# A 48-part projection in a fused two-network kernel: transposing each part by itself instead of twelve parts at a time

## The reference, cut to what matters

```python
def ada_chunks(cvec, w, b):          # cvec: (1024,), w: (1024, 6144), one w per layer
    m = jax.nn.silu(cvec) @ w + b
    return jnp.split(m[..., None, :], 6, axis=-1)
```

## Time and profile before

| | |
|---|---|
| median of 3 runs | 2052.83 us (2052.32 to 2052.91) |
| profiled execution: time, span | 2052.83 us, 2051.0 us |
| PE, PEld busy | 1939.6 us (95%), 1647.2 us (80%) |
| DVE, ACT busy | 1289.0 us (63%), 914.8 us (45%) |
| mean granted TensorE clock | 0.978 of full |

### The profile page before, as it was taken

How to read it: one execution, slowest core, us unless ns; L and a number is a source line. 1 busy time by engine, 2 the same in 40 slices (tenths; PEclk the granted TensorE clock), 3 DMA queues, 4 the chain that set the end, 5 groups by cost and what they waited for, 6 DMA issues and landing times.

```text
span 2051.0 us, 28815 instructions
## 1 busy us (share of the span) xinstructions
PE 1939.6 (95%) x12002; PEld 1647.2 (80%) x12002; DVE 1289.0 (63%) x1732; ACT 914.8 (45%) x1266; POOL 14.2 (1%) x17
## 2 busy tenths in 40 slices
PE   6999978999999999699999998999999989999998
PEld 5788857888788888488779876988888879678997
DVE  4775775776567658667566445665554356757775
ACT  5334534434543353443264345543333254655553
POOL 0000000000000000000000100000000000000000
PEclk9999988999999999899999999999999999999999
DMA  6675444666466644467433311132222222113552
GB/s 264 246 259 194 166 160 163 224 250 228 164 246 226 226 173 176 165 230 265 164 144 131 136 52 52 62 123 83 93 96 99 103 83 86 59 56 130 187 191 95
DMA packets 45488, 320.62 MB, mean 156 GB/s; under 512 B 5040, under 2 KB 5168, under 8 KB 6960
## 3 DMA queue, kind: packets, MB, share of 16 engines
q1 hardware_dynamic: 38592, 270.09, 36.7%
q10 hardware_dynamic: 6768, 48.69, 6.3%
HBM read 317.72 MB, written 1.05 MB: 155 GB/s over the span
## 4 chain that ended last, share of the span: by engine, by line
PE 85%; DVE 9%; ACT 3%; issue 2%; DMA 1%; ACTq 0%; POOLq 0%; POOL 0%; SPq 0%; DVEq 0%
PE ps L521 82%; DVE s_wl L1869 2%; DVE s_big L2147 2%; ACT s_wh L1223 1%; PE ps L858 1%; PE ps L721 0%; DVE s_xx L1869 0%; DVE s_tmp L1956 0%; DMA s_ca<-in_c_all 0%; PE ps L698 0%; DVE s_X L2037 0%; ACT s_xx L1223 0%; DVE s_big L2021 0%; DVE s_tmp L2018 0%; DMA s_big<-in_bias 0%
## 5 line engine op out<-in xcount | busy, mean ns | idle before, releaser
L521 PE MATMUL ps<-s_xx,s_wh 128*128 128x512 f32 (+1 forms) x3328 | 903.5, 349 | 17.4 <-DVE s_wl L1869 16.0
L1869 DVE TENSOR_TENSOR s_wl<-s_raw,s_wh 128x2048 fp32r<-128x2048 f32 x215 | 492.2, 2290 | 334.1 <-ACT s_wh L1223 333.9
L521 PE MATMUL ps<-s_xx,s_wl 128*128 128x256 f32 (+1 forms) x2208 | 671.2, 304 | 7.2 <-DVE s_wl L1869 6.5
L521 PEld LDWEIGHTS ps<-s_xx,s_wh 128*128 128x128 f32 x3328 | 584.1, 191 | 109.9 <-DVE s_wl L1869 19.7
L1223 ACT ACTIVATE s_wh<-s_raw 128x2048 fp32r<-128x2048 f32 x215 | 409.0, 1907 | 158.0 <-PE ps L521 157.6
L521 PEld LDWEIGHTS ps<-s_xx,s_wl 128*128 128x128 f32 x2208 | 421.9, 191 | 25.7 <-DVE s_wl L1869 6.9
L521 PE MATMUL ps<-s_wh,s_hl 128*128 128x512 f32 (+1 forms) x608 | 233.8, 385 | 5.9 <-DVE s_tmp L1956 3.5
L521 PE MATMUL ps<-s_wl,s_hh 128*128 128x512 f32 (+1 forms) x608 | 231.4, 381 | 0.0
L521 PE MATMUL ps<-s_wh,s_hh 128*128 128x512 f32 (+1 forms) x608 | 231.2, 380 | 0.0
L521 PE MATMUL ps<-s_wh,s_xx 128*128 128x256 f32 x928 | 177.6, 286 | 0.0
L521 PEld LDWEIGHTS ps<-s_wh,s_xx 128*128 128x128 f32 x928 | 148.6, 192 | 3.8 <-issue 3.8
(11 more groups left out here) (228 smaller groups left out, 1690.3 us busy)
## 6 DMA issues: line engine op xcount, KB each, us to landing
s_big<-in_w_ada ACTq DMA_DIRECT2D x46, 1024.0 KB, 5.1
s_raw<-in_ffn_gate SPq DMA_DIRECT2D x44, 1024.0 KB, 4.9
s_raw<-in_ffn_up SPq DMA_DIRECT2D x44, 1024.0 KB, 4.8
s_raw<-in_ffn_down SPq DMA_DIRECT2D x44, 1024.0 KB, 4.7
s_raw<-in_w_up SPq DMA_DIRECT2D x44, 1024.0 KB, 4.8
s_raw<-in_w_down SPq DMA_DIRECT2D x22, 1024.0 KB, 4.8
s_raw<-in_w_in SPq DMA_DIRECT2D x18, 1024.0 KB, 4.8
s_raw<-in_w_in_ab SPq DMA_DIRECT2D x10, 1024.0 KB, 4.8
```

Source lines behind the costliest of these rows:

```text
L521: return pe.matmul(o, lhsT, rhs, start=start, stop=stop, skip_group_check=True)
L1869: dve.tensor_tensor(wide(wl, u), raw[:, u % SLOTS, :].rearrange("p (k n) -> p k n", k=8), f32(wide(wh, u)), SUB).then_inc(*w_low.tick(u))
```

## The change

Each part is now transposed by itself. `fill(b)` takes a bank (6 in a feed-forward, the next of the rotation in a mixer) and starts and ends its own accumulation there. `cpad` is a buffer of its own, 32 columns wide, and the slice no longer moves. ACT copies each part to `tmp[:, 5]`, after waiting until the columns of the part before have been taken from it. Directly behind fill f, PE runs `ada_columns(f - 1)`: two matmuls of 128x128 by 128x2 with the constant `pick` (four ones per column). `ada_columns(47)` stays where the last one was, and now also waits for `modulation(0)`. `modulation(0)` waits only for the columns of part 46. The matrix `pick`, and the DVE instruction that made it, are gone. In the mixers `bank()` is called once more for each fill, on PE and on ACT, and `mixer_bank` lists the fills in their places.

```diff
@@ allocation and banks
-        pick = sb("pick", [128, 24])
+        cpad = sb("cpad", [128, 8, 32])
...
-        cpad = big[:, 10816:11248].rearrange("p (k n) -> p k n", k=8)
...
-             ("in", 2), ("rope", "qm"), ("in", 3), ("rope", "km"), "pool", "mean", "stat", "rs"] +
-            [("out", j) for j in range(4)])}
+            [("in", 7), ("in", 8), ("in", 0), ("in", 4), ("in", 5), ("rope", "qd"), ("in", 6), ("rope", "kd"), ("fill", 0),
+             ("fill", 1), ("in", 1), ("in", 2), ("rope", "qm"), ("in", 3), ("rope", "km"), ("fill", 2), "pool",
+             ("fill", 3), ("fill", 4), ("fill", 5), ("fill", 6), "mean", ("fill", 7), "stat", "rs", ("fill", 8)] + [("out", j) for j in range(4)])}
@@ tensor
-            def ada_columns(g):
-
-                pe.wait_ge(*half[g])
-                pe.wait_ge(*picked[0])
+            def ada_columns(f):
+                pe.wait_ge(*half[f])
+                if f == 47:
+                    pe.wait_ge(*modulated[0])
                 for c in range(2):
-                    o = ps[7][:, 48 * g:48 * g + 48].rearrange("p (f c s) -> p f c s", c=2, s=2)[:, :, c, :]
-                    m = mm(o, tmp[:, 5, 128 * c:128 * c + 128], pick[:, :].rearrange("p (f s) -> p f s", s=2), True, True)
-                m.then_inc(*product.tick(("columns", g)))
-
-            def fill():
-
-
+                    m = mm(ps[7][:, 4 * f + 2 * c:4 * f + 2 * c + 2], tmp[:, 5, 128 * c:128 * c + 128], const("pick"),
+                           True, True)
+                m.then_inc(*product.tick(("columns", f)))
+
+            def fill(b):
                 f = fills[0]
                 fills[0] += 1
-                g, i = f // 12, f % 12
+                fill_bank[f] = b
+                pe.wait_ge(*ada_in[f % 2][f])
+                claim(b)
                 if f == 0:
                     pe.wait_ge(*gated["c"])
-                if g and i == 0:
-                    ada_columns(g - 1)
-                pe.wait_ge(*ada_in[f % 2][f])
                 w = ada_buf(f).rearrange("p (k n) -> p k n", k=8)
                 for k in range(8):
                     rows = slice(32 * (k % 4), 32 * (k % 4) + 32)
-                    m = mm(ps[7][rows, 256:512], cpad[:, k, 22 - 2 * i:54 - 2 * i], w[:, k, :], i == 0 and k < 4,
-                           i == 11 and k >= 4)
+                    m = mm(ps[b][rows, 0:256], cpad[:, k, :], w[:, k, :], k < 4, k >= 4)
                 m.then_inc(*product.tick(("fill", f)))
+                freed[b] = half[f]
+                if f:
+                    ada_columns(f - 1)
...
                     if j in ADA_AT[s]:
-                        fill()
+                        fill(6)
                 if s == ("ffn2", 1):
-                    ada_columns(3)
+                    ada_columns(47)
@@ scalar, fill()
-                if f % 12 == 11:
-                    g = f // 12
-                    if g:
-                        act.wait_ge(*product["columns", g - 1])
-                    act.activation(tmp[:, 5, 0:256], ps[7][:, 256:512], ACT.Copy).then_inc(*half.tick(g))
+                if f:
+                    act.wait_ge(*product["columns", f - 1])
+                act.activation(tmp[:, 5, 0:256], ps[fill_bank[f]][:, 0:256], ACT.Copy).then_inc(*half.tick(f))
@@ vector
-                dve.wait_ge(*product["columns", 3])
+                dve.wait_ge(*product["columns", 47 if l else 46])
...
-            dve.tensor_reduce(pick[:, :], const("ident").rearrange("p (g j) -> p j g", g=4)[:, 0:24, :], AX, ADD).then_inc(*picked.tick(0))
```

More of the change, by code:

```diff
@@ L153, in program @@
         normed, hidden, resid, tapped = (signal(n) for n in ("normed", "hidden", "resid", "tapped"))
-        added, picked = signal("added"), signal("picked")
+        added = signal("added")
         roped, masked, row_max, divided = (signal(n) for n in ("roped", "masked", "row_max", "divided"))
@@ L296, in program @@
         k_places = [big[:, 10240:10752], big[:, 10752:11264], cb[:, 768:1280], cb[:, 1280:1792]]
+        fill_bank = {}
         mixer_bank = {x: 6 - n % 2 for n, x in enumerate(
-            [("in", 7), ("in", 8), ("in", 0), ("in", 4), ("in", 5), ("rope", "qd"), ("in", 6), ("rope", "kd"), ("in", 1),
-             ("in", 2), ("rope", "qm"), ("in", 3), ("rope", "km"), "pool", "mean", "stat", "rs"] +
-            [("out", j) for j in range(4)])}
+            [("in", 7), ("in", 8), ("in", 0), ("in", 4), ("in", 5), ("rope", "qd"), ("in", 6), ("rope", "kd"), ("fill", 0),
+             ("fill", 1), ("in", 1), ("in", 2), ("rope", "qm"), ("in", 3), ("rope", "km"), ("fill", 2), "pool",
+             ("fill", 3), ("fill", 4), ("fill", 5), ("fill", 6), "mean", ("fill", 7), "stat", "rs", ("fill", 8)] + [("out", j) for j in range(4)])}
         ropes_flat = ropes[:, :, :].rearrange("p a t -> p (a t)")
@@ L924, in mixer @@
                 for _ in range(2):
-                    fill()
+                    fill(bank())
                 for i in range(6):
@@ L1437, in mixer @@
                 for _ in range(2):
+                    bank()
                     fill()
@@ L1514, in ctx_squares @@
                 act.wait_ge(*ctx_in[0])
-                act.wait_ge(*product["columns", 3])
+                act.wait_ge(*product["columns", 47])
                 for b in range(4):
@@ L1813, in scalar @@
             act.wait_ge(*cleared["cpad"])
-            act.activation(cpad[:, :, 22:24], v("c", 0, 16).rearrange("p (k s) -> p k s", s=2), ACT.Silu).then_inc(
+            act.activation(cpad[:, :, 0:2], v("c", 0, 16).rearrange("p (k s) -> p k s", s=2), ACT.Silu).then_inc(
                 *gated.tick("c"))
```

## The result

The changed kernel took 2071.14 us (median of 4 runs, 2065.65 to 2072.36) beside 2052.57 us for the kernel before on the same chip (2050.53 to 2052.91): 1.0088 times as long, 95% interval 1.0067 to 1.0107. It is slower, by 18.6 us where 13.1 were forecast. Its profiled execution took 2070.3 us with a span of 2068.3, against 2051.0 in the earlier trace rows. PE was busy for 28.6 us more and idle for 11.3 us less, which makes up the 17.3 us by which the span grew.

A forecast was written before the change was run, and what follows sets the result against it. PE, busy for 95% of the span, was taken as the bound. The terms 14.0 + 5.4 - 6.0 - 0.3 = +13.1 us on 2052.83 us gave 2065.9 us, 0.64% slower, range 2059 to 2074.

The forecast's parts named there:

- Part 1: Feed-forwards: 28 more pairs of short matmuls on PE at 0.50 us each, +14.0 us, bounds 9.8 and 15.7.
- Cheap pairs: Rival: a pair's loads hide under running passes, 0.1 us a pair in feed-forwards; +1.9, 2054.7 us; chance 0.08.
- faster: Rival: pairs' loads fit the loader's idle time and copies stay hidden; -6.3, 2046.5 us; chance 0.03.
- Part 2: Five places in each mixer where fills and pairs add time: 2.7 us a mixer, 5.4 for both, bounds 2.8 and 11.6.
- (c): Mixers: one more pair on the way from fill to values, 0.5 us a mixer, up to 1.0 at half clock.
- (d): Mixers, behind fill 13: ACT waits for the pair and copies first, 0.9 us a mixer, up to 1.4.
- (e): Mixers: output projection starts right behind fill 14, so the pair adds 0.5 us a mixer, up to 1.0.
- (a): Mixers: fill 7 waits for the rope's bank, ahead of the scores; 0.1 us a mixer, bounds 0 and 1.5.
- (b): Mixers: pool product moves behind rope "km" on one bank, making DVE late; 0.7 us a mixer, bounds 0 and 0.9.
- the mixers' banks bind: Rival: fills 7 and 8 wait for copies, then PE, DVE, ACT wait at half clock; +19.3, 2072.1 us; chance 0.15.
- Part 3: Before the last feed-forward's down units: PE's 3.52 us wait and the half clock behind it go, -6.0 us.
- Part 4: At the start: DVE's 0.32 us for `pick` leaves the chain, -0.3 us, bounds -0.35 and 0.

The follow-up runs named there:

- e6: Changed kernel without the 29 pairs behind fills in feed-forwards, halves still copied: 2059.24 us, ratio 1.0046 to the kernel before.
- e2: Kernel before with only the end changed: `modulation(0)` waits for fill 47, the last pair waits for `modulation(0)`; no added pairs: 2043.92 us, ratio 0.9968.
- e9: Changed kernel with the pair in front of the fill instead of behind it in feed-forwards: 2062.99 us, ratio 1.0069 to the kernel before.
- e5: Changed kernel with each pair behind a fill in feed-forwards made twice, 29 more pairs: 2078.28 us, ratio 1.0139 to the kernel before.
- e3: Changed kernel with every fill moved to bank 7, out of the mixers' rotation of banks: 2063.43 us, ratio 1.0061 to the kernel before.
- e4: Changed kernel with one bank number skipped in each mixer, ahead of the mean's bank: 2067.71 us, ratio 1.0088 to the kernel before.
- e7: Changed kernel without the 18 pairs behind fills in the mixers: 2059.20 us, ratio 1.0045 to the kernel before.
- e12: Kernel before with the end changed as in e2 and DVE's `pick` sum moved to step 3 of the first feed-forward: 2042.77 us, ratio 0.9969.
- e1: Changed kernel with only the wait put back: `modulation(0)` waits for the last pair of columns again: 2074.20 us, ratio 1.0124 to the kernel before.
- e11: Kernel before measured once more, no edit: 2050.05 us, ratio 1.0005.
- e10: Changed kernel measured once more, no edit: 2063.95 us, ratio 1.0076 to the kernel before.

## Why the prediction was right, and where a size was off

The forecast, slower by 13.1 us to 2065.9, had the right sign, and the median lies in its range. That isn't all merit: the mixers cost more than the forecast's own high bound for them, and part 1 and a pitch that nobody foresaw took 3 us off the other side. On its own terms:

**Part 1, 14.0 us: right, a little high.** At a pitch of 0.353 us the four feed-forwards gained 2.23, 3.59, 3.19 and 193.68 - 189.75 = 3.93 us, in all 12.9, for 28 more pairs: 0.46 each, by the rows 0.45 where 0.50 was taken and 0.35 to 0.56 were the bounds. (Of the 3.93, 0.31 isn't the pairs': e6, without pairs, has 190.06, while e2 is back at the quicker pitch behind its last fill.) The row with eight passes in 1.00 us was a good guide; a pair ahead of a fill costs the 0.34 that the lower bound gave (e9). "Cheap pairs" and "faster", which need 0.1 and 0.05 us a pair, are out: doubling showed 0.45 each (e5). A pass of the pair thus takes 0.112 us at full clock. The Trainium skill ("TensorE: Matmul & The Clock Gate", section "LDWEIGHTS (loading the stationary operand)") puts a load at its columns over 1.2 GHz, 107 ns for 128; the trace agrees within 5% at full clock. At half clock a pair holds PE for 0.88 us, twice as long. The same page's 25 ns floor, which the prediction set beside this rule, doesn't bind here.

**The pitch: not foreseen.** In the first profile ffn2_1 ran at 0.347 us, 1.9 us less than its like. 12.9 - 1.9 - 5.95 = +5.1 is what the four feed-forwards together show. It held through a stage only where pairs stand behind fills, so it looks like an effect of the change that comes in some executions; what sets it isn't shown.

**Part 2, 5.4 us: the term that was too small.** The sum of its five places was the step that failed. The mean over profiles is +12.2 us and the first profile had +14.2, where the high bound was 11.6. (Its low bound doesn't follow from its terms either: (c), (d) and (e) alone have 0.5 + 0.9 + 0.5 = 1.9 a mixer, 3.8 and not 2.8 for both.) DVE has the same instructions in each mixer of every run, so a mixer can be cut at them. The table has the forecast for both mixers and what was measured: the mean of the six profiles with the changed code less that of the four with the code of before. Lines are those of the kernel before.

```
place    the stretch ends with                   forecast  measured
(a)      L2018 for rope "km"                        0.2      +0.94
(b)      L2204, which reads the pool product        1.4      +1.84
(c)      L2215, which reads the mean                1.0      +3.77
(d)      L1886, behind the statistic's products     1.8      +1.45
(e)      L2230, the first residual add              1.0      +1.82
behind   the last turn of x                         0        +2.38
```

(b) and (d) were about right; (b) is 0.92 us in each mixer of all six. Three things are behind the rest. First, the turned rotation was overlooked: PE waits 0.98 us for DVE where the second feed-forward begins, and the stretch is 1.2 us longer each time; e3 and e4 are without it. With (b), banks are 4.2 of the 12.2 us for certain. Second, stretch (c) holds fills 9 to 12 with four pairs, of which one was counted and the others put into PE's waits for DVE and ACT. It cost 2.8 us more than that.

Third, half clock was priced stretch by stretch. PE's busy time can be weighed with the granted clock. In both mixers together PE's work at full clock was 210.4 us with the code of before and 218.6 with the changed code (16 pairs at 0.51), the same within 0.5 us in every profile of a kind. Half clock added 19.3 us to it before (17.2 to 21.7) and 30.1 after (28.3 to 32.1), and PE was idle for 41.5 us before and 34.7 after. So the 12.2 us are 8.2 of work, and 10.8 more from half clock, less 6.8 of idle time. The fall in idle time says that PE's waits did take in part of the pairs, as the forecast had it; a longer half clock more than took that back. Why the half clock lasts longer in the changed code stays open: no run changes it alone. It also moves the cost between places: (a) was at its high bound in mixer 0 of the first profile, +1.55 us, and +0.36 in mixer 1, and (c) took anything from 23.8 to 29.0 us with the same code.

The rival *the mixers' banks bind* gave 2072.1 us and is the nearest in time, but its mechanism is only a part: banks account for 4.2 us and some of (a), by e7 for 3.7 us, of 12.2.

**Part 3, -6.0 us: right.** -5.95 (e2, e12 -5.92) and 6.4 (e1), with the half clock behind the gap as its second half. Against e11, whose own stage was 0.7 us shorter than that of the first profile, e12 is 5.2. The clock was 0.50 behind the gap put back and 1.00 without one, as the prediction's rows had it.

**Part 4, -0.3 us:** the chain starts 0.42 us earlier and the first stage ends 0.59 us earlier, but the start varies by more than that in the runs of before, and e12 didn't show it. "Rest" was -1.39 us in the first profile, -1.43 to +0.13 over all runs with the changed kernel's code there; it isn't a part of the change.

The parts in place of the forecast's: 12.9 + 12.2 - 6.0 - 0.3 = +18.8 us with all products at 0.353 us, and 1.9 us less for each feed-forward at 0.347. The two measured differences were 18.6 (one such feed-forward in the profile) and, for e10, 14.2 us (2063.95 - 2049.78, two of them). The mixers' spread covers what is left.

## What to carry to other kernels

Work that moves from one batch at the end to every step pays its fixed cost each time, so price it from the nearest short passes and multiply; on an engine that is busy for 95% of the time nothing hides it unless a row shows the hole. Where the clock falls behind waits, work added there can be priced only over the whole stage, from several profiles. If a change has a part that gains and a part that costs, look for the gain alone: here one wait needed earlier data, which was already there. When work joins a rotation of buffers, count its uses modulo the rotation, and see who has the last one when the next stage begins.

## What the runs showed of the hardware that wasn't expected

- The same stream of 512- and 256-column passes runs at one of two pitches, 0.353 or 0.347 us a pair of passes, at a granted clock of 1.00. A pitch holds over many steps and changes at a stage's beginning or behind a fill. A feed-forward is 1.9 us shorter at the quicker one (198.87 and 200.79 us). Of the 18 later feed-forwards without a pair behind their fills none kept the quicker pitch past the first fill; of 24 with such pairs 9 did. What picks it is open.
- One and the same mixer code took 136.4 to 142.7 us in six profiles (mixer 1 of the changed kernel's code), with the half clock lying now on PE's work, now on its waits (shown for two of them: 142.66 and 137.70 us).
- Four 128x2 passes with their loads cost 0.45 us behind the 16 passes of a fill (32 columns wide, in four column groups) and 0.34 us ahead of them.
